# Memory cross-attention of a decoder trunk: squares on ScalarE, query rows handed over one at a time, four score banks in place of two

## The reference, cut to what matters

```
q = rms_norm((h @ wq).reshape(B, S, XA_HEADS, XA_HEAD_DIM), q_norm)
k = rms_norm((mem_h @ wk).reshape(B, M, XA_HEADS, XA_HEAD_DIM), k_norm)
v = (mem_h @ wv).reshape(B, M, XA_HEADS, XA_HEAD_DIM)
s = jnp.einsum('bshd,bmhd->bhsm', q, k).astype(jnp.float32) * (XA_HEAD_DIM ** -0.5)
p = jax.nn.softmax(s, axis=-1)
o = jnp.einsum('bhsm,bmhd->bshd', p.astype(v.dtype), v).reshape(B, S, XA_WIDTH)
return o @ wo
```

## Time and profile before

| | before |
|---|---|
| median of 3 runs | 2300.04 us (2299.57 to 2300.17) |
| the profiled execution | 2299.59 us, span 2297.8 us |
| mean granted TensorE clock | 0.987 |
| PE, PEld busy | 96%, 84% of the span |
| DVE, ACT, POOL busy | 60%, 51%, 76% |
| stream | 367.12 MB, mean 160 GB/s |

### The profile page before, as it was taken

One profiled execution on the slowest core, in us unless ns is written; L12 is line 12 of the kernel. 1 busy time (PEld: TensorE's weight loads), 2 busy tenths in 40 slices (PEclk: granted clock), 3 DMA queues, 4 the chain that ended last, 5 costly groups with the idle time before them and its releaser, 6 DMA issues.

```text
span 2297.8 us, 51292 instructions
## 1 busy us (share of the span) xinstructions
PE 2196.9 (96%) x15526; PEld 1938.4 (84%) x15530; DVE 1382.3 (60%) x2291; ACT 1168.2 (51%) x2273; POOL 1750.8 (76%) x1316
## 2 busy tenths in 40 slices
PE   6999979999999999999979999899999999999998
PEld 5787868999999888888868877699999998888887
DVE  3444547994666788733346445489756667886333
ACT  5445654555444455456544455545554444555564
POOL 4745846998777788888867458469988777888886
PEclk9999999999999999999999999999999999999999
DMA  6423424555444444465554235235454444455554
GB/s 241 147 92 110 156 97 137 173 170 178 160 159 161 156 171 166 164 208 186 192 202 154 91 105 175 95 135 179 166 174 163 156 164 156 168 170 182 193 191 148
DMA packets 100517, 367.12 MB, mean 160 GB/s; under 512 B 11472, under 2 KB 11984, under 8 KB 100176
## 3 DMA queue, kind: packets, MB, share of 16 engines
q1 hardware_dynamic: 97040, 353.41, 45.3%
q10 hardware_dynamic: 3392, 12.66, 1.5%
HBM read 364.98 MB, written 1.05 MB: 159 GB/s over the span
## 4 chain that ended last, share of the span: by engine, by line
PE 45%; DVE 2%; issue 2%; ACT 1%; POOL 1%; POOLq 0%; DVEq 0%; ACTq 0%
PE acc L1067 5%; PE acc L1068 5%; PE acc L1069 5%; PE acc L1096 5%; PE acc L1098 5%; PE acc L1097 5%; PE acc L806 3%; PE acc L808 3%; PE acc L807 3%; PE aux L1035 2%; PE aux L768 1%; POOL w_lo L453 1%; PE aux L853 0%; PE aux L918 0%; DVE h_lo L1159 0%
## 5 line engine op out<-in xcount | busy, mean ns | idle before, releaser
L453 POOL TENSOR_TENSOR w_lo<-raw,w_hi 128x512 fp32r<-128x512 f32 x1312 | 1750.6, 1348 | 534.7 <-ACT w_hi L499 439.5
L499 ACT ACTIVATE w_hi<-raw 128x512 fp32r<-128x512 f32 x1344 | 841.7, 629 | 818.7 <-PE acc L1069 424.5
L1067 PE MATMUL acc<-h_hi,w_hi 128*128 128x256 f32 x2048 | 587.0, 287 | 9.7 <-POOL w_lo L453 9.7
L1068 PE MATMUL acc<-h_lo,w_hi 128*128 128x256 f32 x2048 | 579.3, 283 | 0.0
L1069 PE MATMUL acc<-h_hi,w_lo 128*128 128x256 f32 x2048 | 579.1, 283 | 0.0
L1096 PE MATMUL acc<-w_hi,eg 128*128 128x512 f32 x1024 | 406.2, 397 | 1.2 <-DVE eg L1628 1.2
L1067 PEld LDWEIGHTS acc<-h_hi,w_hi 128*128 128x128 f32 x2048 | 392.0, 191 | 12.7 <-POOL w_lo L453 12.6
L1098 PE MATMUL acc<-w_hi,eg 128*128 128x512 f32 x1024 | 399.6, 390 | 0.0
L1097 PE MATMUL acc<-w_lo,eg 128*128 128x512 f32 x1024 | 398.7, 389 | 0.0
L1068 PEld LDWEIGHTS acc<-h_lo,w_hi 128*128 128x128 f32 x2048 | 392.4, 192 | 0.1
L1069 PEld LDWEIGHTS acc<-h_hi,w_lo 128*128 128x128 f32 x2048 | 392.1, 191 | 0.0
(11 more groups left out here) (231 smaller groups left out, 2190.1 us busy)
## 6 DMA issues: line engine op xcount, KB each, us to landing
raw<-stream_dram SPq DMA_DIRECT2D x672, 512.0 KB, 3.3
big<-parb_dram ACTq DMA_DIRECT2D x2, 2128.0 KB, 9.6
big<-mem_dram ACTq DMA_DIRECT2D x3, 1024.0 KB, 5.6
big<-pm_dram ACTq DMA_DIRECT2D x2, 768.0 KB, 13.4
big<-parr_dram ACTq DMA_DIRECT2D x2, 640.0 KB, 10.6
X<-x_dram ACTq DMA_DIRECT2D x1, 1024.0 KB, 12.1
out_dram<-X SPq DMA_DIRECT2D x1, 1024.0 KB, 4.0
big<-lnrow_dram ACTq DMA_DIRECT2D x2, 256.0 KB, 11.4
```

What stands on the lines that cost most here:

```text
L453: nc.gpsimd.tensor_tensor(w_lo[:, k % SLOTS, :], raw[:, k // PER_CHUNK, k % PER_CHUNK, :], w_hi[:, k % SLOTS, :].bitcast(F32), ALU.subtrac ...
L499: nc.scalar.activation(w_hi[:, k % SLOTS, :], raw[:, (k // PER_CHUNK) % RAW, k % PER_CHUNK, :], ACT.Copy).then_inc(hi_ready, 1)
L1067: pe_.matmul(acc[:, q, 0:S], wh, h_hi[:, kt, :], start=(kt == 0), stop=False)
L1068: pe_.matmul(acc[:, q, 0:S], wh, h_lo[:, kt, :], start=False, stop=False)
```

## The change

It does five things in the middle of the cross-attention.

- The query rows are handed over one row tile at a time: the first copy out of `acc` signals `xq_rows`, the second ends the block. `xq_T0` and `xq_T1` are now the four heads of one row tile each.
- ACT squares each row tile (`xsquare`, signal `xq_square`), and DVE sums each one by head. The one large multiplication on DVE is gone.
- DVE copies the transposed queries of tile 0 ahead of the sum of tile 1, and both ahead of the wait for ACT's root.
- An exponential of one column is put behind the root on ACT.
- Each of the four units has a bank, a place in `xring` and `xpT` and a place for its maxima (`xmx`). PE issues all four units' scores, then `xp_T0`, and then by turns `xp_T{u+1}` and the value matmuls of u. DVE takes the maxima of units 0 to 2 ahead of the first copy of transposed exponentials, and makes both divisions at the end.

```diff
-USES += [("xs0", 0), ("xs1", 1)]
-for _u in range(len(XUNITS)):
-    USES += [(f"xp_T{_u}", 2)]
-    if _u + 2 < len(XUNITS):
-        USES += [(f"xs{_u + 2}", _u % 2)]
-    if _u % 2 == 0:
-        USES += [(f"xo_{_u // 2}", 3)]
-USES += [("xo_T0", 0), ("xo_T1", 1)]
+USES += [(f"xs{u}", u) for u in range(len(XUNITS))] + [(f"xp_T{u}", u) for u in range(len(XUNITS))]
+USES += [("xo_0", 0), ("xo_1", 2), ("xo_T0", 1), ("xo_T1", 3)]
...
@@ ACT
                 hi(3)
+                for t in range(T):
+                    if t == 0:
+                        a.wait("xq_rows")
+                    else:
+                        a.wait_block("xq")
+                    a.step(nc.scalar.activation(xsquare[:, t, :], xqt[:, t, :], ACT.Square), "xq_square")
                 root(ssh[:, 0:8], "xq_mean", "xq_sqrt")
+                a.step(nc.scalar.activation(st[:, 94:95], ident[:, 0:1], ACT.Exp))
...
@@ PE
-                e.wait_block("xq")
-                for i in range(2):
-                    transposes(f"xq_T{i}", [xqt[:, t, h * XD:(h + 1) * XD] for h in (2 * i, 2 * i + 1) for t in range(T)])
+                for t in range(T):
+                    if t == 0:
+                        e.wait("xq_rows")
+                    else:
+                        e.wait_block("xq")
+                    transposes(f"xq_T{t}", [xqt[:, t, h * XD:(h + 1) * XD] for h in range(XH)])
...
+                e.wait_block("mem_v")
+                for u in range(len(XUNITS)):
+                    e.wait_drained(f"xq_T{XUNITS[u][0]}")
+                    xscores(u)
+                xprobs(0)
+                for u in range(len(XUNITS)):
+                    if u + 1 < len(XUNITS):
+                        xprobs(u + 1)
+                    xvalues(u)
...
@@ DVE
-                read_block("xq", [(t, 0, COL, xqt[:, t, :]) for t in range(T)], ssx)
-
-                xqh = xqt.rearrange("p t (h c) -> p (t h) c", c=XD)
-                d.step(V.tensor_tensor(tmph, xqh, xqh, ALU.mult))
-                d.step(V.tensor_reduce(ssh[:, 0:8], tmph, AX.X, ALU.add))
-                mean(ssh[:, 0:8], XD, "xq_mean")
-                d.wait("xq_sqrt")
-                for i in range(2):
-                    use = f"xq_T{i}"
+                d.wait_pieces(LAST["xq"])
+                for t in range(T):
+                    d.step(V.tensor_scalar(xqt[:, t, :], acc[:, PARITY["xq"] * 2 + t, :], ssx[:, t:t + 1], None, ALU.mult),
+                           **(dict(block="xq") if t else dict(name="xq_rows")))
+                for t in range(T):
+                    d.wait("xq_square", t + 1)
+                    d.step(V.tensor_reduce(ssh[:, 4 * t:4 * t + 4], xsquare[:, t, :].rearrange("p (h c) -> p h c", c=XD), AX.X, ALU.add))
+                    if t:
+                        mean(ssh[:, 0:8], XD, "xq_mean")
+                    use = f"xq_T{t}"
                     d.wait_filled(use)
...
+                for u in range(3):
+                    x_scores(u)
+                x_probs(0)
+                x_scores(3)
+                for u in range(1, 4):
+                    x_probs(u)
+                for t in range(T):
+                    d.wait_drained(f"xs{2 * t + 1}")
+                    d.step(V.reciprocal(coef[:, 0:4], sums[:, t, 0:4]))
```

More of the change, by code:

```diff
@@ L132 @@
 REUSE = {"zq": ("memx", 0), "sg": ("memx", 1024), "rawd": ("mk", 0), "dT": ("mk", 0), "o": ("knd", 0),
[L133 removed]
+         "junk": ("kTm", 0), "merged": ("w1", 0), "xo": ("gates", 4096), "pq": ("gates", 0), "pqT": ("gates", 2048), "xring": ("gates", 0), "xpT": ("gates", 2048),
          "sring": ("KV2", 0), "pT": ("blk", 0), "yT": ("vn", 0), "vblk": ("lnrow", 0),
@@ L220, in trunk @@
         pT = region("pT", 1024, 2, 4, 128)
+        xring = region("xring", 2048, 4, 2, MEM)
+        xsquare = region("xring", 1024, T, COL)
+        xpT = region("xpT", 2048, 4, 4, P)
         vblk = region("vblk", 512)
@@ L290, in trunk @@
         cmx = st[:, 58:74]
+        xmx = st[:, 58:66].rearrange("p (u h) -> p u h", u=4)
         sums = st[:, 74:90].rearrange("p (r h) -> p r h", r=2)
@@ L319, in trunk @@
             s_ready=len(UNITS), p_exp=len(UNITS), o_ready=1, merged_ready=2,
+            xq_rows=1, xq_square=T,
             xq_mean=1, xq_sqrt=1, xs_ready=len(XUNITS), xo_ready=1,
@@ L624, in _ @@
                     for h in range(2):
-                        a.step(nc.scalar.activation(sring[:, u % 2, h, :], bank(f"xs{u}")[:, h * MEM:(h + 1) * MEM],
-                                                    ACT.Exp, scale=ssh[:, 4 * t + 2 * j + h:4 * t + 2 * j + h + 1], bias=nmx[:, u % 2, h:h + 1],
+                        a.step(nc.scalar.activation(xring[:, u, h, :], bank(f"xs{u}")[:, h * MEM:(h + 1) * MEM],
+                                                    ACT.Exp, scale=ssh[:, 4 * t + 2 * j + h:4 * t + 2 * j + h + 1], bias=xmx[:, u, h:h + 1],
                                                     accum_out=sums[:, t, 2 * j + h:2 * j + h + 1]),
@@ L977, in xscores, with xprobs, xvalues @@
                     fill(ins, f"xs{u}")
[L979 to L983, removed]
+                def xprobs(u):
                     e.wait_drained(f"xs{u}")
-                    transposes(f"xp_T{u}", [sring[:, u % 2, h, c * P:(c + 1) * P] for h in range(2) for c in range(2)])
-                    if u + 2 < len(XUNITS):
-                        xscores(u + 2)
+                    transposes(f"xp_T{u}", [xring[:, u, h, c * P:(c + 1) * P] for h in range(2) for c in range(2)])
+                def xvalues(u):
+                    t, j = XUNITS[u]
                     e.wait_drained(f"xp_T{u}")
@@ L994, in _ @@
                             at = (2 * j + h) * XD
-                            ins = pe_.matmul(bank(use)[:, at:at + XD], pT[:, u % 2, h * 2 + c, :],
+                            ins = pe_.matmul(bank(use)[:, at:at + XD], xpT[:, u, h * 2 + c, :],
                                              mv[:, c, at:at + XD], start=(c == 0), stop=(c == 1))
@@ L1471, in _ @@
                 add_rows("out", "xa", C_XA, 2)
-                read_block("xq", [(t, 0, COL, xqt[:, t, :]) for t in range(T)], ssx)
-                xqh = xqt.rearrange("p t (h c) -> p (t h) c", c=XD)
-                d.step(V.tensor_tensor(tmph, xqh, xqh, ALU.mult))
-                d.step(V.tensor_reduce(ssh[:, 0:8], tmph, AX.X, ALU.add))
-                mean(ssh[:, 0:8], XD, "xq_mean")
-                d.wait("xq_sqrt")
-                for i in range(2):
-                    use = f"xq_T{i}"
+                d.wait_pieces(LAST["xq"])
[8 more added lines that the diff above has]
+                    use = f"xq_T{t}"
                     d.wait_filled(use)
-                    d.step(V.tensor_scalar(xqT[:, 2 * i:2 * i + 2, :], bank(use).rearrange("p (j s) -> p j s", j=2),
+                    d.step(V.tensor_scalar(xqT[:, :, t * P:(t + 1) * P], bank(use).rearrange("p (h s) -> p h s", h=XH),
                                            col[:, C_XQN:C_XQN + 1], None, ALU.mult), drains=use)
@@ L1491, in x_scores, with x_probs @@
                     d.wait_filled(f"xs{u}")
-                    m = nmx[:, u % 2, :]
+                    m = xmx[:, u, :]
                     d.step(V.tensor_reduce(m, bank(f"xs{u}").rearrange("p (h m) -> p h m", h=2), AX.X, ALU.max, negate=True))
                     d.step(V.tensor_tensor(m, m, ssh[:, 4 * t + 2 * j:4 * t + 2 * j + 2], ALU.mult), "xs_ready")
-                x_scores(0)
-                x_scores(1)
-                for u, (t, j) in enumerate(XUNITS):
+                def x_probs(u):
                     use = f"xp_T{u}"
                     d.wait_filled(use)
[L1501 to L1511, removed]
+                    d.step(V.tensor_copy(xpT[:, u], bank(use).rearrange("p (n s) -> p n s", n=4)), drains=use)
+                for u in range(3):
[7 more added lines that the diff above has]
+                    d.step(V.reciprocal(coef[:, 0:4], sums[:, t, 0:4]))
+                    d.wait_filled(f"xo_{t}")
+                    d.step(V.tensor_tensor(xo[:, t, :].rearrange("p (h c) -> p h c", h=4),
+                                           bank(f"xo_{t}").rearrange("p (h c) -> p h c", h=4),
+                                           coef[:, 0:4].unsqueeze(2).broadcast_to((P, 4, XD)), ALU.mult),
+                           drains=f"xo_{t}")
                 sig["xo_ready"].sent += 1
```

## The result

The changed kernel takes 2286.69 us (median of 5, 2284.66 to 2289.84) against 2300.17 us (2299.57 to 2302.43) before: ratio 0.9944, 95% interval 0.9933 to 0.9955. It is 13.5 us faster, near the forecast of 2285.0 and inside the range.

The account below looks back on a forecast made before the run. The prediction took a serial chain from engine to engine in the middle of cross-attention as the bound; 7.50 us less a layer, 15.0 in both, gave 2284.6 for the profiled execution, 2285.0 as median, range 2282.5 to 2291.

Parts of the forecast that it names:

- Rows handed over singly: PE's query transposes: both tiles done by 297.35, half a microsecond earlier; alone worth nothing, since what follows waits for DVE.
- the sum: The chain worked through at the high clock: 7.50 us less a layer, 15.0 in both, 2284.6 for the profiled execution.
- Squares on ACT, two sums of 0.69: DVE's row up to the scale: loses multiplication (2.14 us) and sum (1.22), gets two sums of 0.69; gain 2.28 us.
- Exponential behind the root: ACT, behind the hidden table load: an added exponential of about 0.20 us costs nothing, with 0.3 us of cover.
- rival B: ACT's first exponential waits further behind the table load, until about 302.3: about 0.8 us later a layer, 2286.6; chance 0.04.
- Four banks, scores ahead: Unit loop: early scores, ACT's exponentials without holes; output's transposes at 310.49, not 317.99, 7.50 us less a layer.
- Both divisions last: End of DVE's unit work: row tile 0's division (0.18 and 0.69) runs during values 2 and 3, costing nothing.
- Case C, the gain taken back by the stream: Behind the stage: the weight stream sets the pace, so `xo0` begins earlier and then stalls; 2300; chance 0.04.
- The clock: PE's clock stays high throughout the stage, its hole before the scores 0.9 us instead of 4.41; main doubt, forecast's chance 0.62.
- case A: Clock falls at the scores as before: 5.0 us less a layer, 2290.0; shorter stretch costs 1.3 a layer, 2287.6; chance 0.22.
- case D: PE's small work stays at half speed to the stage's end and into `xo0`: 2 to 4 us more a layer, 2306; chance 0.03.
- Case E: Unit loop: waits hold units apart as before, only DVE's shorter work counts: 2.3 us a layer, 2295.4; chance 0.05.

Follow-up runs that it names:

- the fillers: Matmuls of zeros in PE's holes: changed kernel 2285.51 us, stage 17.96; kernel before 2300.69 us, stage 24.46; also in kernels with only part of the change.
- the front alone: Kernel before plus single row handover, ACT's squares and exponential, DVE's new order up to the root; old unit loop and banks: 2297.34 us, ratio 0.9992.
- the kernel before, with fillers: Kernel before plus 17 matmuls of zeros in PE's hole between query transposes and first scores: 2300.69 us, ratio 1.000.

## Why the prediction was right, point by point

- **Rows handed over singly.** Right: all transposes of queries ended 0.4 us earlier (2.25 us after the queries, where it was 2.68). "That alone is worth nothing" was too little for what the same handover allows later: unit 0's scores on tile 0, 0.82 us a layer, was in the sum, but under the four banks.
- **Squares on ACT, two sums of 0.69.** The sum took 0.69; the squares ended at 1425.77 and 1426.55, before DVE asked. The scale ended 5.20 us after the queries, against 5.19 forecast. The step is 2.27 us (2.28 forecast).
- **Exponential behind the root.** Cost nothing, with 0.30 us of cover as worked out, and is worth nothing. The row behind the load (1428.71, 1.28 us, next activation at 1430.01) shows no further wait, so rival B and the drain of the Trainium skill (ScalarE: Activation LUTs, What ACT_TABLE_LOAD costs) do not appear in this case.
- **Four banks, scores ahead.** At the high clock the output's transposes start 15.50 us after the queries, against 15.36; the stage is 17.96 us against 17.9. The 0.14 is ACT's pace: the sum had 1.39 us from one unit's exponentials to the next, and they start every 1.46 (1430.51, 1431.97, 1433.42), so that PE's second transposes start 9.10 us after the queries and not 8.94.
- **Both divisions last.** Row tile 0's division lay beside the last values; nothing was late.
- **Case C, the gain taken back by the stream.** Did not occur in the profiled execution: from `xo0` of layer 0 to the queries of layer 1 it took 1111.0 us, before 1111.1.
- **The clock.** This is the step that failed. The sum had "the high level throughout", with 0.62; the profiled executions show a low stretch at or behind each stage of the changed kernel, three times of three. What came in layer 0 is case A's shorter stretch, and it cost 0.6 us in the stage, not 1.3. The clock fell 0.5 us behind the start of unit 0's scores, but DVE asks for them only when its scale is done, so the first exponential still came at 6.16; then unit 1's maximum was 0.9 us late, its exponentials 0.4 and the output's transposes 0.6. And outside of case D I looked for it inside the stage alone: in layer 1 it came 17 us after the queries and cost 1.4 us on `xo0`. The two together are 2.0 us, and the sum of 2284.6 for the profiled execution becomes 2286.6 with them; it took 2286.28, with its start 0.4 us shorter. The other two samples, 2284.80 and 2286.81 us, lie on both sides of the forecast of 2285.0, so how near a single median comes to the forecast is, within 2 us, luck. Of the 7.50 us a layer in the sum 6.50 are the chain, as the fillers show, and 0.94 are the low clock of the old stage. The first part stood in every comparison at the high clock; of the second, something was taken back wherever a low stretch was left in or behind a stage.
- **Case D, slower by the clock.** Did not occur. Something like its mechanism shows in another kernel: the front alone had the clock low for 10.2 us, and it came back inside the stage.
- **Case E.** Its price, 2.3 us a layer for the front, is right at an equal clock (2.28) and wrong at the granted one (0.3 to 0.5).

## What to carry to other kernels

Where a serial chain between engines stands on the path, a timeline walked through operation by operation, with the handovers of 0.03 to 0.1 us, gave the new length within 1% here, at the high clock; what a part is worth can depend on another part (here 0.82 us a layer came only with both, since an early operand helps only if its consumer doesn't wait for the late one too). A stage with holes on TensorE has a second price, the low clock behind it, and shortening or filling the holes may only move it onto other work (the kernel before, with fillers) or may take it away (the front alone): judge such edits by the length of the stage at one clock, and by several runs of the whole.

## What had not been expected of the hardware

The clock's low stretches in and behind these stages lasted 3.4, 6.8 or 10.2 us, and where one falls differs between executions of the same kernel: at the start of the scores, or 17 us later. In the first profile of the changed kernel PE had done thin work ahead of each fall: 1.67 us in 3.4 with two holes of 0.84 and 0.94 us in layer 0, 1.73 us in layer 1. But in the kernel before it did as little, 1.67 us in 3.5 from 312.50, and the clock stayed at 1.00, so thin work does not by itself tell where a fall comes. With matmuls of zeros in the holes it was at 1.00 in each stage in which they stood.
